# Gates' projection ahead of the sliding keys and values in the last layer of a three-layer transformer kernel

## The reference, cut to what matters

```python
def hybrid_layer(x, norm_g, w_in, ...):
    h = rms_norm_2(x, norm_g)
    proj = h @ w_in
    (q, kc, vc, ks, vs, kw, vw, gl, g_nsa, rwkv_in, g_rwkv) = _split(proj, IN_SIZES)
    o_nsa = nsa_mixer(q, kc, vc, ks, vs, kw, vw, gl, ...)
...
def nsa_mixer(q, kc, vc, ks, vs, kw, vw, gate_logits, ...):
    k_cmp = compress_blocks(kvh(kc), pos_k, w1_k, w2_k)     # silu(flat @ w1) @ w2
    v_cmp = compress_blocks(kvh(vc), pos_v, w1_v, w2_v)
    ...
    g = jax.nn.sigmoid(gate_logits)
    o = g[..., 0:1] * o_cmp + g[..., 1:2] * o_sel + g[..., 2:3] * o_win
```

## Time and profile before

| what | value |
|---|---|
| time, median of 3 runs | 1192.33 us (1189.94 to 1192.78) |
| profiled execution, its own time | 1190.88 us |
| its span, first to last instruction | 1189.1 us |
| PE busy | 1130.8 us, 95% of the span |
| PEld / DVE / ACT / POOL busy | 947.9 / 596.3 / 507.6 / 417.3 us |
| mean granted TensorE clock | 0.990 of full |

### The profile page before, as it was taken

The page is one execution under the profiler, slowest core; times in us unless marked ns, Lnnn a source line. Parts: engine busy times, 40 slices in busy tenths (PEclk is TensorE's granted clock), DMA queues, the critical chain, the costliest instruction groups (busy, mean ns, idle before and its releaser), DMA issues.

```text
span 1189.1 us, 24304 instructions
## 1 busy us (share of the span) xinstructions
PE 1130.8 (95%) x10103; PEld 947.9 (80%) x10103; DVE 596.3 (50%) x1312; ACT 507.6 (43%) x1025; POOL 417.3 (35%) x363
## 2 busy tenths in 40 slices
PE   3999999999999999899999999988999999999996
PEld 3998888799998998656699998966777787677763
DVE  5000001872327347798723439027874897345646
ACT  4232222973424432488824345343884521122221
POOL 4734574776335445400153335230006342000000
PEclk9999999999999999999999999999999999999998
DMA  7432343323222223200042223352002223100001
GB/s 219 148 99 80 106 105 108 99 56 100 72 72 71 92 87 106 71 1 2 1 142 72 72 71 125 107 159 71 2 2 71 71 72 115 55 31 3 4 2 71
DMA packets 73335, 89.57 MB, mean 75 GB/s; under 512 B 2017, under 2 KB 66666, under 8 KB 73098
## 3 DMA queue, kind: packets, MB, share of 16 engines
q1 hardware_dynamic: 70136, 78.12, 20.5%
q0 software_dynamic: 2416, 8.26, 2.9%
q10 hardware_dynamic: 674, 1.64, 0.5%
HBM read 83.75 MB, written 4.26 MB: 74 GB/s over the span
## 4 chain that ended last, share of the span: by engine, by line
PE 83%; DVE 6%; ACT 4%; DMA 2%; POOL 2%; issue 1%; ACTq 1%; DVEq 0%; POOLq 0%
PE bank L477 76%; PE bank L804 2%; POOL ring_parts L2699 2%; ACT arena L1380 1%; PE bank L714 1%; DMA arena<-x_kept 1%; PE bank L1003 1%; ACT ring_parts L1409 1%; PE bank L569 1%; ACT arena L1761 1%; ACT arena L1496 1%; DMA vrow<-in_final_norm_g 1%; DVE arena L2422 0%; ACTq L1375 0%; DMA ring<-in_cmp_w_v 0%
## 5 line engine op out<-in xcount | busy, mean ns | idle before, releaser
L2699 POOL TENSOR_TENSOR ring_parts<-ring,ring_parts 128x512 fp32r<-128x512 f32 (+1 forms) x236 | 308.8, 1341 | 431.7 <-ACT ring_parts L1409 340.7
L477 PE MATMUL bank<-ring_parts,arena_parts 128*128 128x256 f32 x1856 | 322.1, 283 | 0.0
L477 PEld LDWEIGHTS bank<-ring_parts,arena_parts 128*128 128x128 f32 x1856 | 271.4, 190 | 1.7 <-issue 1.3
L477 PE MATMUL bank<-hT_parts,ring_parts 128*128 128x512 f32 x704 | 234.4, 395 | 0.0
L477 PE MATMUL bank<-arena_parts,ring_parts 128*128 128x512 f32 x640 | 223.5, 399 | 2.8 <-POOL ring_parts L2699 2.8
L477 PE MATMUL bank<-ring_parts,hT_parts 128*128 128x256 f32 x1024 | 221.1, 283 | 3.8 <-POOL ring_parts L2699 2.9
L1380 ACT ACTIVATE arena<-bank 128x512 f32<-128x512 f32 (+5 forms) x287 | 135.0, 539 | 191.8 <-PE bank L477 171.0
L477 PEld LDWEIGHTS bank<-ring_parts,hT_parts 128*128 128x128 f32 x1024 | 170.6, 191 | 5.0 <-POOL ring_parts L2699 3.7
L477 PE MATMUL bank<-arena 64*64 64x64 f32 (+7 forms) x1904 | 163.4, 316 | 7.9 <-ACT arena L1761 2.9
L477 PEld LDWEIGHTS bank<-hT_parts,ring_parts 128*128 128x128 f32 x704 | 133.0, 189 | 31.2
L477 PEld LDWEIGHTS bank<-arena_parts,ring_parts 128*128 128x128 f32 x640 | 121.5, 190 | 31.5 <-ACT arena L1380 3.0
(11 more groups left out here) (271 smaller groups left out, 1409.9 us busy)
## 6 DMA issues: line engine op xcount, KB each, us to landing
ring<-in_a_w_in SPq DMA_DIRECT2D x16, 1024.0 KB, 5.5
ring<-in_w_in SPq DMA_DIRECT2D x15, 1024.0 KB, 5.5
ring<-in_b_w_in SPq DMA_DIRECT2D x10, 1024.0 KB, 5.0
ring<-in_ple_w_gate SPq DMA_DIRECT2D x8, 1024.0 KB, 5.2
arena<-rpb_rows POOLq DMA_DIRECT2D x16, 256.0 KB, 3.5
ring<-in_a_w_out SPq DMA_DIRECT2D x4, 1024.0 KB, 5.3
ring<-in_b_w_out SPq DMA_DIRECT2D x4, 1024.0 KB, 5.3
ring<-in_w_out SPq DMA_DIRECT2D x4, 1024.0 KB, 5.1
```

The costliest lines, as they stand in the source:

```text
L477: return nc.tensor.matmul(o, l, r, start=start, stop=stop)
L2699: nc.gpsimd.tensor_tensor(rounded(r), r, read_back(high_slot(n)[:, o:o + m // 4]), ALU.subtract)\
```

## The change

In the list of loads Cbg comes ahead of Cwin. PE does bg ahead of the four tiles of win. ACT's third call of `high` names the block that is now the last of the two; since `high` walks the list, it covers the same place in the list as before. DVE's program, POOL's and the order in which ACT drains win and bg stay as they are.

```diff
-                           ("Cwin", 1024, 1280), ("Cbg", 1280, 1408)):
+                           ("Cbg", 1280, 1408), ("Cwin", 1024, 1280)):
             load(name, cols(w_in2, a, b), (KB, b - a))
...
             tokens(("Cq", 1), "q1")
-            tokens("Cwin", "win")
             need3("Cbg")
             fm3("bg", "v", "Cbg", 0, act2)
             used3("Cbg")
+            tokens("Cwin", "win")
...
-            high(HI["Cbg"])
+            high(HI["Cwin"])
             keys_values(1, "win")
             evacuated(act, "bg")
```

## The result

| what | before | after |
|---|---|---|
| median of 20 runs | 1190.82 us (1188.47 to 1194.51) | 1194.39 us (1192.37 to 1196.91) |
| ratio, with its 95% interval | | 1.0030 (1.0022 to 1.0038) |
| profiled execution, its own time | 1190.88 us | 1192.37 us |

What follows compares the result with a forecast made beforehand. PE was taken to bound the kernel, so its new idleness counts in full: 2.55 (wait) + 0.1 (restart) + 1.5 (clock) = +4.15 us on 1192.33, forecast 1196.5 us, range 1193.0 to 1198.9.

Steps and rivals of the forecast that it cites:

- The preparation behind q1: Ahead of win: its parts, complete at 762.91, come after bg's cover ends at 760.50; PE newly waits 2.55 us for POOL.
- PE's own work: In win and bg: the same matmuls issued in the other order, 16.86 us together; cost 0.
- bg's preparation: Bg as fifth block: lowering ends near 748.5, 6.4 us ahead of need; cost 0.
- ACT's and DVE's queues: Behind win: bg's tanh and DVE's rotations end later but stay covered, by 2.2 and 3.9 us; early bg gains nil.
- The loads: Behind bg and the pair: earlier (W1K,1) gains 0; PE's 1.03 us wait for (W1V,1) stays; bounds -1.03 to +0.5.
- Rival D: Second half of "hid": (W1V,1) arrives earlier, PE's 1.03 us wait goes; 1191.3 us if C holds too; chance 0.05.
- POOL beside DVE: In win's lowering: bg's scaling on DVE doesn't stretch POOL; taken as 0, bounds 0 to +1.42 us.
- Rival B: In win's lowering: DVE and POOL hinder each other, +1.42 us on top, +5.6 and 1197.9 us; chance 0.07.
- TensorE's clock: Behind the new wait: the granted clock falls to half; 0 or +1.5 to +1.7 us, taken as +1.5.
- Rival A: Behind the new wait: the clock does not fall; +2.65 us, 1195.0 us; chance 0.32.

Runs made afterwards that it cites:

- after_quarters: Kernel after, but PE waits for POOL's first quarter only ahead of win, and for each further quarter where it first reads it; 1191.54 us, ratio 0.9995.
- look_b: The changed kernel with no edit, one more execution for a profile of the clock behind the new wait; 1197.46 us.
- both_early: Kernel before with ACT's `high` for (Cog,0) one tile earlier and, in hid's second half, (W1K,1)'s eight matmuls ahead of (W1V,1)'s; 1190.53 us, ratio 0.9995.
- pe_only: Kernel before with only PE's order exchanged, bg ahead of win; list of loads and ACT's call left as before; 1203.44 us, ratio 1.0098.

## Why the prediction was right, and where it was not

The direction, the place and the wait's size were right, and so was the total: +4.15 us forecast, +3.6 measured (2.6 to 4.5), and the median in the range. That the total fits so well is in part luck: 1.5 us of the forecast are a fall of the clock that mostly doesn't come, and some 1.0 of the measured 3.6 are falls that lie elsewhere for the most part. The forecast in us was 2.1 too high, of which 1.5 come from before itself: its median over 20 runs is 1190.82, and over the three it was given by 1192.33.

- **The preparation behind q1.** Right. PE started win 7.75 us behind q1's end (761.73 against 753.98) where the sum said 7.90. The difference is the handing over from POOL to PE, 0.05 us instead of 0.14, and POOL's 4.98 for 5.04. The wait between the starts is 2.4 us instead of 2.55, and after_quarters shows that the cost goes with it.
- **PE's own work, bg's preparation, ACT's and DVE's queues.** Costed at nothing, and nothing they cost. bg is lowered by 747.6. ACT's tanh ends at 774.59, 1.2 us behind win's end, and DVE's rotations at 778.61, 5.3 behind (1.4 and 5.2 were said). No wait of PE for either is in the profile between 750 and 800 us.
- **The loads.** Right in kind: (W1K,1) at bg's end gains nothing, and the wait for (W1V,1) stays. It is 0.15 us shorter, the transfer taking 5.34 us instead of 5.49. The wait itself is 0.78 to 1.01 us in the six profiles, 1.03 in before. Rival D's mechanism is there with a seventh of its price.
- **POOL beside DVE.** Rival B is refuted: the four quarters took 4.98 us with bg's scaling (0.68 us) inside them. The Trainium skill's rule ("SBUF — State Buffer", section "SBUF: two separate sides"), that a DVE operation hinders GpSimd only with two SBUF inputs or in a two-port mode, agrees with it.
- **TensorE's clock.** This step failed, though the sum survived it. The forecast took a fall behind the new wait as the likelier case, at 0.6 to 0.4; it was seen in one profile of six, and at 0.6 a count so low has a chance of 4%. Its size was right (1.5 us), so on average it brings a quarter of a microsecond. Rival A, the wait without the fall, is the case that most profiles show. The step that went wrong is the reading of the earlier trace rows: from one profile it took it that some idle times bring a fall and others don't, by their length. The fourteen profiles show that each brings it in a part of the executions, and the shortest, the 1.8 us at 390 us, in half of them. The Trainium skill's rule ("TensorE: Matmul & The Clock Gate", section "HAM oscillation — how this bites in real kernels"), by which so short a gap leaves the clock up, holds behind the new wait in five profiles of six and fails in look_b; at 390 us it fails in seven of fourteen.
- **What stays open.** The wait and the small drift behind it make 2.5 to 2.7 us in the profiles; the average difference is 3.6 (interval from 2.6). By the six profiles the missing 0.9 us are falls of the clock, a quarter of it the one behind the wait and the rest at later places. The mean granted clocks agree in size, 0.9885 for the changed kernel and 0.9892 for before, which is 0.8 us more lost. But that difference, 0.0007, is less than twice its standard error of 0.0004, and before was profiled only once. So it isn't settled whether such falls come more often with the change or only came so in these executions.

## What to carry to other kernels

When two blocks of different size change places in a pipelined order, ask what each has for cover: here the preparation of the block behind q1 takes 7.8 us if wide and 4.7 if narrow, and the narrow block's own matmuls cover only 5.6. Here the narrow block belongs behind the wide one, ahead of work that needs no preparation. If the order must be the other, let the consumer wait for pieces and not for the whole: four waits instead of one took the 2.2 us down to 0.2.

Whether TensorE's clock falls behind a wait can't be read from one profile. Look at the same wait in several executions, and put the fall into the sum with the share in which it came, not as a yes or no.

## What the runs showed of the hardware that was not expected

- Matmuls that alternate between the two halves of a bank's partitions (64 output partitions each) ran at 0.12 us a record; the same ones with eight of one half in a row took 6.3 us for 32 records, 0.20 each. The order of both_early thus cost 2.6 us to save a wait of 1.0. The Trainium skill has a reason that fits ("TensorE: Matmul & The Clock Gate", section "The mechanism"): matmuls on different tiles of the array overlap. The section draws it for tiles that differ in their rows, and these differ in their columns. No run here separates it from other reasons.
- Whether the clock falls behind a given wait differs between executions of one kernel: behind the same 2.2 us it fell in one profile of six, behind the same 1.8 us at 390 us in seven of fourteen, and behind the 2.84 us at the output gate in ten of eleven (not in after_quarters). Behind 4.7 us (pe_only) it was at half in the one profile taken, for 6.8 us.
- Eighteen more matmuls at 759 us came with 1.5 us of idle PE at 1153 us that no releaser explains; nine did not. An experiment that adds instructions has to be read to its end.
